# Latent tokens laid out by grid columns: neighbourhood scores over 288 instead of 384 keys, biases and mask over 160 instead of 256 latent keys

## The reference, cut to what matters

```
def neighbourhood_attention(q, k, v, k_ctx, v_ctx, rpb, scale):
    ...
    col_start = jnp.clip(q_cols - NA_WIN_W // 2, 0, GRID_W - NA_WIN_W)
    col_ok = (kc >= col_start[..., None]) & (kc < col_start[..., None] + NA_WIN_W)
    ...
    bias = jnp.where(col_ok[None, None], bias.astype(jnp.float32), NEG_INF)
    s_loc = jnp.einsum('bjqhd,bajkhd->bhjqak', q_r, k_blk).astype(jnp.float32) * scale + bias
    s_ctx = jnp.einsum('bjqhd,blhd->bhjql', q_r, k_ctx).astype(jnp.float32) * scale
    p = jax.nn.softmax(jnp.concatenate([s_loc, s_ctx], axis=-1), axis=-1)
    o = (jnp.einsum('bhjqak,bajkhd->bjqhd', p_loc, v_blk)
         + jnp.einsum('bhjql,blhd->bjqhd', p[..., n_loc:], v_ctx))
```

## Time and profile before

| | |
|---|---|
| median of 3 runs | 1314.19 us (1313.23 to 1314.57) |
| the profiled execution | 1313.9 us, of it span 1312.0 us |
| PE busy (matmul) | 1287.5 us, 98% |
| DVE busy | 785.9 us, 60% |
| ACT busy | 515.0 us, 39% |
| POOL busy | 61.0 us, 5% |
| granted clock of TensorE | 0.998 |

### The profile page before, as it was taken

How to read it: one execution, slowest core, us unless ns; L and a number is a source line. 1 busy time by engine, 2 the same in 40 slices (tenths; PEclk the granted TensorE clock), 3 DMA queues, 4 the chain that set the end, 5 groups by cost and what they waited for, 6 DMA issues and landing times.

```text
span 1312.0 us, 16948 instructions
## 1 busy us (share of the span) xinstructions
PE 1287.5 (98%) x6563; PEld 1021.8 (78%) x6563; DVE 785.9 (60%) x1139; ACT 515.0 (39%) x880; POOL 61.0 (5%) x80
## 2 busy tenths in 40 slices
PE   5999999999999999999999999999999999999997
PEld 2556677888888878888887788887888888888885
DVE  3344765875766767764876477884454444454445
ACT  4224243344334333354333834333443434333333
POOL 0000300000100010000001100000000000000000
PEclk9999999999999999999999999999999999999999
DMA  9999787455666367635776566663332212216553
GB/s 379 394 407 405 276 307 266 143 154 192 227 211 204 129 208 244 201 123 197 274 273 212 192 218 202 231 213 120 113 97 65 64 50 65 65 53 245 152 154 135
DMA packets 70111, 257.80 MB, mean 197 GB/s; under 512 B 8504, under 2 KB 8632, under 8 KB 68752
## 3 DMA queue, kind: packets, MB, share of 16 engines
q1 hardware_dynamic: 64224, 234.96, 52.2%
q0 software_dynamic: 5520, 21.17, 4.9%
q10 hardware_dynamic: 288, 0.59, 0.1%
HBM read 248.76 MB, written 7.93 MB: 196 GB/s over the span
## 4 chain that ended last, share of the span: by engine, by line
PE 78%; DVE 3%; issue 1%; ACT 1%; POOL 0%; DVEq 0%; ACTq 0%; POOLq 0%
PE gemm L530 17%; PE gemm L532 16%; PE gemm L531 16%; PE attended L736 3%; PE turned L686 3%; PE gemm L502 2%; PE gemm L504 2%; PE gemm L503 2%; PE scores L992 2%; PE scores L996 1%; PE scores L722 1%; PE ada_bank L532 1%; PE ada_bank L530 1%; PE ada_bank L531 1%; DVE w_lo L1475 1%
## 5 line engine op out<-in xcount | busy, mean ns | idle before, releaser
L530 PE MATMUL gemm<-w_hi,act_lo 128*128 128x512 f32 x1146 | 459.6, 401 | 0.9 <-DVE act_lo L1487 0.5
L1475 DVE TENSOR_TENSOR w_lo<-w_raw,w_hi 128x1024 fp32r<-128x1024 f32 x241 | 297.6, 1239 | 271.2 <-ACT w_hi L1068 270.4
L532 PE MATMUL gemm<-w_hi,act_hi 128*128 128x512 f32 x1146 | 447.5, 391 | 0.0
L531 PE MATMUL gemm<-w_lo,act_hi 128*128 128x512 f32 x1146 | 446.7, 390 | 0.0
L1068 ACT ACTIVATE w_hi<-w_raw 128x1024 fp32r<-128x1024 f32 x241 | 252.5, 1055 | 295.3 <-PE gemm L532 244.3
L530 PEld LDWEIGHTS gemm<-w_hi,act_lo 128*128 128x128 f32 x1146 | 215.4, 188 | 54.0 <-issue 11.8
L532 PEld LDWEIGHTS gemm<-w_hi,act_hi 128*128 128x128 f32 x1146 | 215.1, 188 | 46.5
L531 PEld LDWEIGHTS gemm<-w_lo,act_hi 128*128 128x128 f32 x1146 | 215.6, 188 | 42.3
L1128 ACT ACTIVATE prob<-scores,nmax 128x384 f32<-128x384 f32 (+1 forms) x96 | 48.9, 510 | 102.1 <-DVE nmax L1668 95.8
L1668 DVE TENSOR_REDUCE nmax<-scores 128x1 f32<-128x384 f32 (+1 forms) x96 | 42.6, 466 | 69.3 <-PE scores L996 48.5
L1561 DVE SCALAR_TENSOR_TENSOR ada<-ada,silu_c 128x1024 f32<-128x1024 f32 x62 | 81.3, 1349 | 0.0
(11 more groups left out here) (336 smaller groups left out, 1568.0 us busy)
## 6 DMA issues: line engine op xcount, KB each, us to landing
w_raw<-in_w_all SPq DMA_DIRECT2D x245, 512.0 KB, 3.8
ada<-in_ada_all SPq DMA_DIRECT2D x160, 512.0 KB, 6.7
gate_ring<-in_ada_all SPq DMA_DIRECT2D x24, 512.0 KB, 4.5
gate_bc<-gate_scratch POOLq DMA_DIRECT2D x4, 1024.0 KB, 7.3
st<-x_scratch POOLq DMA_DIRECT2D x4, 768.0 KB, 4.9
x_scratch<-u POOLq DMA_DIRECT2D x3, 768.0 KB, 4.6
u<-in_x_sample SPq DMA_DIRECT2D x2, 1024.0 KB, 8.2
bias<-in_bias_all POOLq DMA_DIRECT2D x2, 1024.0 KB, 8.7
```

Of the source, the lines that this page charges most:

```text
L530: pe.matmul(bank_[:], alo, whi[:, kk], start=first, stop=False)
L531: pe.matmul(bank_[:], ahi, wlo[:, kk], start=False, stop=False)
L532: last = pe.matmul(bank_[:], ahi, whi[:, kk], start=False, stop=end)
L1475: dve.tensor_tensor(w_lo[:, r, 0:width], w_raw[:, r, 0:width], hi_slot(w)[:, 0:width].bitcast(F32), ALU.subtract).then_inc(lo_ready, 1)
```

## The change

The latent tokens are put in the order of grid columns: four rows of a column stand together. Tile t = 1 holds columns 31 down to 0, tile t = 2 columns 32 up to 63. A query of tile 1 then sees no key beyond its own tile and the first 32 tokens of tile 2 (columns 32 to 39), and the other way round (columns 31 to 24). `BESIDE` = 32, `OWN` = 160, `NEAR` = 288. The host reorders x_sample, the rotary tables, the biases and the mask, and puts y_sample back.

- `near_score`: t = 1 is one product of 288 columns (cache, own block, 32 keys beside); t = 2 is two, of 160 (cache and the 32 beside) and of 128 (own).
- `near_turn`: the third of the three transposes for t = 1, 2 has 32 columns of probabilities instead of 128, and fills 32 partitions.
- `near_attend`: of the three products for t = 1, 2 the middle one sums over 32 rows instead of 128.
- VectorE adds bias over 160 columns and takes the maximum over 288; ScalarE's exponential is over 288. The copies to `probT` stay at 384 columns.
- bias is 128x1280 for a stage instead of 128x2048; mask is 128x320 instead of 128x64 and lies in the room left over by bias.

```diff
+            def near_score(n, h, t):
+                need(pe, p_ready, n - 1)
+                s, query = S[n % 2], qT[:, h, t * P:(t + 1) * P]
+                if t == 0:
+                    last = pe.matmul(s[:, 0:P], query, kT[:, h, 0:P], start=True, stop=True)
+                elif t == 1:
+                    last = pe.matmul(s[:, 0:NEAR], query, kT[:, h, P:P + NEAR], start=True, stop=True)
+                else:
+                    pe.matmul(s[:, 0:OWN], query, kT[:, h, P:P + OWN], start=True, stop=True)
+                    last = pe.matmul(s[:, OWN:NEAR], query, kT[:, h, 3 * P:KEYS], start=True, stop=True)
+                last.then_inc(s_done, 1)
+            def near_turn(n, t, tau):
...
+                own, beside = (P, 2 * P) if t == 1 else (OWN, P)
+                turn(TB, [p[:, 0:P], p[:, own:own + P]])
+                pe.transpose(TB[0:BESIDE, 2 * P:3 * P], p[:, beside:beside + BESIDE], ident[:])\
+                    .then_inc(t_done, 1)
+            def near_attend(n, t, tau, h):
...
+                    pe.matmul(out, probT[:, n % 2, 0:P], v4[:, 1, cols], start=True, stop=False)
+                    pe.matmul(out, probT[0:BESIDE, n % 2, 2 * P:3 * P], v4[0:BESIDE, 4 - t, cols],
+                              start=False, stop=False)
+                    last = pe.matmul(out, probT[:, n % 2, P:2 * P], v4[:, 1 + t, cols], start=False, stop=True)
+                last.then_inc(pv_done, 1)
...
-                score(n0 + (n + 2), (n + 2) // NT, (n + 2) % NT, (n + 2) // NT)
+                near_score(n0 + (n + 2), (n + 2) // NT, (n + 2) % NT)
...
-                width = P if t == 0 else 3 * P
+                width = P if t == 0 else NEAR if biased else 3 * P
...
-                    own.add(dve.tensor_tensor(
-                        s[:, P:3 * P], s[:, P:3 * P],
-                        bias[:, h, t - 1, :, :].rearrange("p r c -> p (r c)"), ALU.add))
+                    own.add(dve.tensor_tensor(s[:, P:NEAR], s[:, P:NEAR], bias[:, h, t - 1, :], ALU.add))
...
-                flat = bias[:].rearrange("p h q r c -> p (h q r) c")
-                pool.tensor_tensor(flat, flat, spread(mask[:], [[0, 8 * GROUP], [1, GRID_W]]), ALU.add)\
+                flat = bias[:].rearrange("p h q n -> p h (q n)")
+                pool.tensor_tensor(flat, flat, spread(mask[:], [[0, GROUP], [1, 2 * OWN]]), ALU.add)\
...
+def token_order():
+    column, row = np.meshgrid(np.arange(GRID_W), np.arange(4), indexing="ij")
+    token = row * GRID_W + column
+    return np.concatenate([token[GRID_W // 2 - 1::-1].reshape(-1), token[GRID_W // 2:].reshape(-1)])
```

More of the change, by code:

```diff
@@ L38 @@
 ROPE = 64
+BESIDE = P // 4
+OWN = P + BESIDE
+NEAR = P + OWN
 SLOT = 1024
@@ L228, in build @@
         bias_at = top[0]
-        bias = sb("bias", [P, GROUP, 2, 4, GRID_W])
+        bias_room = sb("bias_room", [P, 4, CH])
+        bias = sb("bias", [P, GROUP, 2, OWN], at=bias_at)
+        mask = sb("mask", [P, 2, OWN], at=bias_at + 2 * GROUP * OWN * 4)
+        assert 2 * (GROUP + 1) * OWN <= 4 * CH
         gain_ql = sb("gain_ql", [P, CH], at=bias_at)
@@ L240, in build @@
         cos1 = sb("cos1", [P, 2, ROPE]); sin1 = sb("sin1", [P, 2, ROPE])
-        mask = sb("mask", [P, GRID_W])
         ident = sb("ident", [P, P])
@@ L723, in score @@
                           start=True, stop=True).then_inc(s_done, 1)
+            def near_score(n, h, t):
[10 more added lines that the diff above has]
+            def near_turn(n, t, tau):
+                need(pe, p_ready, n + 1)
+                need(pe, t_free, tau)
+                p = prob[:, n % 3, :]
+                if t == 0:
+                    turn(TB, [p[:, 0:P]]).then_inc(t_done, 1)
+                    return
+                own, beside = (P, 2 * P) if t == 1 else (OWN, P)
[3 more added lines that the diff above has]
+            def near_attend(n, t, tau, h):
+                need(pe, t_free, tau + 1)
+                need(pe, o_done, n)
+                out = OB[:, n % 4 * P:(n % 4 + 1) * P]
+                cols = slice(h * P, (h + 1) * P)
+                if t == 0:
+                    last = pe.matmul(out, probT[:, n % 2, 0:P], v4[:, 0, cols], start=True, stop=True)
+                else:
+                    pe.matmul(out, probT[:, n % 2, 0:P], v4[:, 1, cols], start=True, stop=False)
[3 more added lines that the diff above has]
+                last.then_inc(pv_done, 1)
             def prob_turn(n, t, tau):
@@ L827, in _ @@
                             pe.wait_ge(x_free, X_U0 + EARLY)
-                        score(n0, 0, 0, 0)
-                        score(n0 + 1, 0, 1, 0)
+                        near_score(n0, 0, 0)
+                        near_score(n0 + 1, 0, 1)
                     chunk_slot((w0 + j), j % SPC, m + (NT * (j // SPC)))
@@ L852, in attend_b @@
                     h = n // NT
-                    attend(n0 + n, n % NT, tau + (2 * GROUP + n),
-                           lambda kt: v4[:, kt, h * P:(h + 1) * P])
+                    near_attend(n0 + n, n % NT, tau + (2 * GROUP + n), h)
                 for n in range(UNITS):
-                    prob_turn(n0 + n, n % NT, tau + (2 * GROUP + n))
+                    near_turn(n0 + n, n % NT, tau + (2 * GROUP + n))
                     if n + 2 < UNITS:
-                        score(n0 + (n + 2), (n + 2) // NT, (n + 2) % NT, (n + 2) // NT)
+                        near_score(n0 + (n + 2), (n + 2) // NT, (n + 2) % NT)
                     if n > 0:
@@ L1121, in evacuate_gate, with exponent @@
                     act.activation(stage[1][:, t, :], banks[t][:], ACT.Tanh, scale=0.5).then_inc(evac, 1)
-            def exponent(n, t):
-                width = P if t == 0 else 3 * P
+            def exponent(n, t, full=3 * P):
+                width = P if t == 0 else full
                 need(act, mx_ready, n + 1)
@@ L1247, in _ @@
                     if j == 3 * SPC - 1:
-                        exponent(n0, 0)
-                        exponent(n0 + 1, 1)
+                        exponent(n0, 0, NEAR)
+                        exponent(n0 + 1, 1, NEAR)
                     if 2 <= j < 6:
@@ L1268, in _ @@
                     if n + 2 < UNITS:
-                        exponent(n0 + (n + 2), (n + 2) % NT)
+                        exponent(n0 + (n + 2), (n + 2) % NT, NEAR)
                     if n == 0:
@@ L2192, in _ @@
                 pool.dma_start(v4[:, 1, :], vc[:, slice(i * CH, i * CH + CH)]).then_inc(vc_in, 16)
-                pool.dma_start(bias[:].rearrange("p h q r c -> p (h q r c)"), t_in["bias_all"][i])\
+                pool.dma_start(bias[:].rearrange("p h q n -> p (h q n)"), t_in["bias_all"][i])\
                     .then_inc(bias_in, 16)
                 pool.wait_ge(bias_in, 16 * (i + 1))
-                flat = bias[:].rearrange("p h q r c -> p (h q r) c")
-                pool.tensor_tensor(flat, flat, spread(mask[:], [[0, 8 * GROUP], [1, GRID_W]]), ALU.add)\
+                flat = bias[:].rearrange("p h q n -> p h (q n)")
+                pool.tensor_tensor(flat, flat, spread(mask[:], [[0, GROUP], [1, 2 * OWN]]), ALU.add)\
                     .then_inc(bias_ready, 1)
@@ L2314, in lay_out @@
         arrays[name] = f[name]
-    token = np.arange(2 * P)
+    token = token_order()
+    arrays["x_sample"] = np.ascontiguousarray(f["x_sample"][:, token])
     for n, width in ((0, HEAD), (1, ROPE)):
@@ L2324, in lay_out @@
                 table.astype(np.float32).reshape(2, P, width).transpose(1, 0, 2))
-    col = np.arange(P)[:, None] % GRID_W
+    query = token.reshape(2, P)[:, :, None]
+    keys = np.stack([token[0:OWN], np.concatenate([token[0:BESIDE], token[P:2 * P]])])[:, None]
+    col, key = query % GRID_W, keys % GRID_W
     start = np.clip(col - WIN // 2, 0, GRID_W - WIN)
-    key = np.arange(GRID_W)[None]
-    arrays["mask"] = np.where((key >= start) & (key < start + WIN), 0.0, -1e30).astype(np.float32)
-    query, keys = np.arange(2 * P)[:, None], np.arange(2 * P)[None]
+    arrays["mask"] = np.ascontiguousarray(
+        np.where((key >= start) & (key < start + WIN), 0.0, -1e30).astype(np.float32).transpose(1, 0, 2))
     dy = keys // GRID_W - query // GRID_W + 2 * 4 - 1
-    dx = np.clip(keys % GRID_W - query % GRID_W + WIN - 1, 0, 2 * WIN - 2)
+    dx = np.clip(key - col + WIN - 1, 0, 2 * WIN - 2)
     arrays["bias_all"] = np.ascontiguousarray(
-        f["l0_rpb"][:, dy, dx].reshape(N_B, GROUP, 2, P, 2 * P).transpose(0, 3, 1, 2, 4)
-        .reshape(N_B, P, GROUP * 2 * 2 * P))
+        f["l0_rpb"][:, dy, dx].reshape(N_B, GROUP, 2, P, OWN).transpose(0, 3, 1, 2, 4)
+        .reshape(N_B, P, GROUP * 2 * OWN))
     arrays["ident"] = np.eye(P, dtype=np.float32)
@@ L2358 @@
     r = run_bass_kernel_spmd(nc, [{f"in_{n}": a for n, a in arrays.items()}], core_ids=[0])
-    return tuple(r.results[0][f"out_{n}"] for n, _ in OUTS)
+    out = {n: r.results[0][f"out_{n}"] for n, _ in OUTS}
+    out["y_sample"] = np.ascontiguousarray(out["y_sample"][:, np.argsort(token_order())])
```

(1 more changed line is left out.)

## The result

The changed kernel takes 1317.47 us, median of 11 runs (1316.91 to 1318.62), against 1314.24 us of the kernel before beside it (11 runs, 1313.23 to 1315.98). The ratio is 1.0024, 95% interval 1.0016 to 1.0032: slower, by some 3.2 us. The forecast was 1317.5 us, 3.3 us more than before.

What follows compares the result with a forecast made beforehand. TensorE, busy 98% of the span, was taken to bound the kernel. Scores -2.5, stall -0.4 and the 32-row product +6.2 sum to +3.3 us on a 1314.19 median: 1317.5 us, 8-in-10 range 1313.5 to 1319.5.

Steps and rivals of the forecast that it cites:

- TensorE alone is the limit in the two stages: Stages 0 and 1: TensorE busy 57.00 of 57.00 and 37.79 of 38.00 us, so its instructions' gains or losses reach the time.
- Scores, 2.5 us saved: Score products for t = 1, 2: fewer columns save 0.16 us in each of 16 units, 2.5 us in all.
- Narrow turn, nothing: Third transpose: its moving operand still has 128 columns, so the pass stays at 0.11 us and nothing is gained.
- rival that gave it a visit of its own: Third transpose over 32 columns costs 0.3 us in each of 16 units, 4.9 us more, 1322.4 us; chance 0.08.
- Product over 32 rows, 0.39 us a visit, 6.2 us: Middle attended product: 0.09 in, 0.09 out and two open loads of 0.10 add 0.39 us a unit, 6.2 us.
- free form: Rival: the attended product over 32 rows adds nothing, so the kernel is 2.9 us faster, 1311.3 us; chance 0.12.
- half the price: Rival: the product over 32 rows costs only 0.09 us each way, loads hidden; 2.9 us added, 1314.2 us; chance 0.12.
- upper bound: Product over 32 rows: 0.45 us a unit, 7.2 us, if the second product behind recovers 0.05 us late too.
- The stall of stage 1, 0.4 us saved: Stage 1: TensorE's 0.38 us wait for VectorE's u before an attended product goes, some 0.4 us saved in all.
- what was left to spare: At that stage 1 wait: u would be ready with about 0.8 us to spare before TensorE needs it.
- GpSimd: Bias sum shrinks from 4.61 us; it and the loads are done at 333 us, 78 us before the units reading them.
- Sum: Whole kernel: -2.5 - 0.4 + 6.2 = +3.3 us, giving 1317.5 us, 0.25% slower; chance of this case 0.68.

Runs made afterwards that it cites:

- wide scores: Changed kernel with scores of 384 columns in one product for t = 1 and 2, as before the change: 1319.89 us, ratio 1.0040 to the kernel before.
- full rows: Changed kernel with the middle attended product over all 128 rows instead of 32, the other rows stale: 1311.69 us, ratio 0.9979 to the kernel before.
- wide turn: Changed kernel with the third transpose over 128 columns and partitions instead of 32: 1317.66 us, ratio 1.0024 to the kernel before.
- full rows, old widths: Changed kernel with the middle attended product over 128 rows, bias over 256 columns, maximum and exponential over 384: 1311.91 us, ratio 0.9982 to the kernel before.

## Why the prediction was right, point by point

- *TensorE alone is the limit in the two stages.* Right. Stages and total moved by TensorE's own instructions; nothing behind stage 1 took anything back (708.01 and 707.94 us). One reading was off: the list of waits does hold something over 0.5 us after the start, 0.6 for qT. It stands in both kernels and at 263 us, ahead of the stages, so that nothing follows from it.
- *Scores, 2.5 us saved.* Right: 16 * 0.158 = 2.5, by the experiment with wide scores. The kernel with full rows against the one before says the same in stage 0: 1.30 us for eight units, 0.16 each.
- *Narrow turn, nothing.* Right: 0.11 in the chain, and the wide turn changes no stage by more than 0.04 us. The rival that gave it a visit of its own is out.
- *Product over 32 rows, 0.39 us a visit, 6.2 us.* Right: 0.385 from stage 0 with full rows and 1.05 - 0.67 = 0.38 from the chain. Its four parts stand in the timeline as they were read from the 64\*128 products of layer 1 in the earlier trace rows: 0.09 in, an open load, 0.09 out, an open load. The rivals of a free form and of half the price are out; 32 rows, 64 rows, in the middle and last cost the same, and a second one in the same visit only its passes. That nothing is loaded ahead of a change of rows is seen in the loads of L766 and L768. What happens inside TensorE is not seen in a trace: that it first finishes what it has in it is a reading that fits the 0.09, no more. (The upper bound is 0.39 + 0.05 = 0.44, hence 7.0 us; the prediction writes 0.45 and 7.2.)
- *The stall of stage 1, 0.4 us saved.* Right in size and cause, with a slip in what was left to spare. Counted from the start of stage 1, u ends at 15.91 us before, at 15.45 with the shorter scores alone (full rows, old widths) and at 15.02 in the changed kernel: 0.46 and 0.43 earlier, forecast 0.47 and 0.4. The two visits delay TensorE by 0.77 (it could start at 15.04 with full rows, at 15.81 in the changed kernel), forecast 0.8. But TensorE has four shorter scores on its own way there, which make it 0.63 earlier (15.67 before, 15.04 with full rows), and the prediction doesn't name them. So the spare time is 0.46 + 0.43 + 0.77 - 0.63 - 0.38 = 0.65 us: in the changed kernel u ends at 584.52, TensorE could start 0.14 later, at 584.66, and comes at 585.31. The forecast of 0.8 isn't the sum of its own terms (0.4 + 0.47 + 0.8 - 0.38 = 1.3), so that it lies near 0.65 is luck; the time doesn't depend on it. The kernel with full rows and old widths has 0.53 us of stall at that product, and the one with full rows alone 0.14.
- *GpSimd.* Right: the bias sum of stage 0 takes 2.94 us instead of 4.61 and is done at 330 us, far ahead of the stage.
- *Sum.* Stages +1.78 and +1.40 = 3.18 us against 3.3, measured 3.2.

The chances had put 0.12 each on the free form and on half the price. Both deserved less: the trace of before held a price at two other forms, and the one row for a free form was of fewer columns, not of fewer rows.

## What to carry to other kernels

On an engine that is busy all the time, a smaller product isn't a cheaper one: count passes and moving columns first, then changes of form. Fewer moving columns paid to the ns, fewer stationary columns or rows paid nothing, and a product over fewer rows between full ones cost 0.39 us, nearly two plain products' worth. Where a sum has a short rest block, fill it up with zeros that are written once, and keep the form.

## What was not expected

- A turn of form 128\*32 at column 0 is free (0.11 us), while products of the same form at four column positions step in with 0.09. Whether the positions or something else about these products makes the difference, no run here shows. For rows it is otherwise: one product at row 0 alone pays the full visit.
- The stages repeat to 0.04 us between kernels in which they are equal, while the stretch ahead of them moves by 1.8 us (410.78 to 412.55) and the medians with it by some tenths. Where the question is a few tenths of a us, cut the traces at the same instructions instead of comparing totals.
